# Gate tiles of stick-breaking attention read x before its norm factor, and the second split of x moves behind them

## The chip, the cores and the metric

The kernel runs on one core of a Trainium2 chip. The metric is the device time of one execution in microseconds, the median of several runs. All times below are in microseconds unless they are marked otherwise. A stretch such as "174 to 200" is counted from the first instruction of the profiled execution.

## What is computed

x has 512 tokens of 1024 features, in fp32. A first block has three branches from one normed x: a pooling mixer, a gated linear recurrence and a stick-breaking attention, each weighted by a sigmoid gate. A feed-forward follows, and then two more layers of attention and feed-forward, which the change does not touch. What the change touches is this part of the reference:

```python
h = rms_norm(x, norm_mix[l])                       # x * rsqrt(mean(x*x)) * norm_mix
proj = jnp.einsum('bsd,dc->bsc', h, w_in[l])
u_pool, u_lru, q, k, v, g_logits = jnp.split(proj, splits, axis=-1)
gates = jax.nn.sigmoid(g_logits + b_gate[l]).reshape(B, S, N_BRANCH, D_MODEL)
y_pool = pool_mixer(u_pool, ...)
y_lru = rglru_mixer(u_lru, ..., lru_lambda[l])
qh, kh = rms_norm(q per head), rms_norm(k per head)
y_sb = stick_breaking_attention(qh, kh, vh)        # softplus of the scores, sums along the keys, exp
merged = gates[0]*(y_pool @ w0) + gates[1]*(y_lru @ w1) + gates[2]*(y_sb @ w2)
```

## The kernel before, in words

**Products.** Every fp32 product is made of three matmuls with fp32r operands: each operand is held as a high part and a low part (its rest), and low by high, high by high and high by low are summed in PSUM (lines 313 to 315, `products`). One tile is 128 features by 512 tokens, over 8 slices of the 1024 input features, so 24 matmuls.

**Weights.** They come in chunks of 1 MB. SyncE fetches a chunk into `raw` when GpSimd has finished with the chunk two places earlier. ScalarE makes the high part (line 973, `refill`), in the order of its own program and after the PE has finished with the buffer. GpSimd makes the low part in four pieces (line 853), and the PE waits for each piece. There are two buffers, so a chunk that is refilled late meets the PE two tiles or more later. A chunk holds two tiles of 128 features.

**x.** The first split of x has the gain `norm_mix` but not the factor 1/rms of the token (`rstd`), which isn't known yet. The 16 query and key tiles (feature by token) and the values (token by feature) are made from it, and `rstd` or its transposed copy is applied to the sums. Then the second split is made: VectorE writes x times gain times `rstd` (`x_normed`, line 1601), ScalarE copies it to the high part (`normed`, line 1146), VectorE subtracts (`x_low`, line 1607). The kernel before does this for tiles 0 to 3 between the last value tiles, where the PE has finished with the slices, and for tiles 4 to 7 right after them. Everything later in the block reads the second split.

**Query projection.** For each of 16 tiles the PE makes the product; VectorE scales it (line 1537); ScalarE squares it (line 1136); VectorE splits the square in two (lines 1546 and 1548); and the PE sums it over the features (`qk_sum`, line 536) after the product of a later tile. The buffers of the squares are two deep. ScalarE's refills stand between its squares in one program.

**Values.** Two halves (i), each of two chunks (c) and four token tiles (b). After the first half's first chunk, ScalarE refills, then takes a square root for the norm of q and k (line 1154), then copies the values out of banks 0 to 3 (line 1159), which the second half needs. Between these, VectorE and ScalarE compute small terms from `diff_lambda` and `lru_lambda` (the decay terms, lines 1560 to 1580). In the second half the PE spreads the norm factors (`qk_spread`, line 582) and VectorE applies them (line 1593).

**Attention.** Eight heads. For each head h the PE runs, in this order: the gate tile `sb_gate(h)` (a `g2x` tile, 24 matmuls into bank 7), the scores of head h+1 (line 626), the values of head h-1 (line 652), and the sums of head h (`sb_sums`, lines 638 and 642). ScalarE and VectorE make softplus from the scores (lines 1178 to 1184, and 1628 to 1640, which ends in `sp_ready`); `sb_sums` waits for it. VectorE reads bank 7 after that (line 1645). Before the first head the PE makes the scores of heads 0 and 1. After the last sums come `lru(0)`, the values of head 7, `lru(1)`, and the attention's branch product `sb_branch(0)`.

**Behind it.** Recurrence and branch tiles, then eight pooling tiles, then `g0x` 0 and 1, the pool product (`wp`), and `g0x` 2 and 3, whose chunk ScalarE refills with `mix_refill(16)`; each has a number n in the list `MIX`.

The order on the PE at the start of attention, which the change leaves as it is:

```python
            sb_scores(0)
            sb_scores(1)
            sb_gate(0)
            sb_sums(0)
            for h in range(1, 7):
                sb_gate(h)
                sb_scores(h + 1)
                sb_values(h - 1)
                sb_sums(h)
            sb_gate(7)
            sb_values(6)
            sb_sums(7)
            lru(0)
```

## Time and profile before

| what | before |
|---|---|
| median of 3 runs | 2308.89 us (2307.97 to 2309.07) |
| the profiled execution's own time | 2308.41 us |
| its span, first to last instruction | 2306.7 us |
| PE matmul busy | 2236.3 us (97%) |
| PE weight load busy | 1812.0 us (79%) |
| GpSimd, VectorE, ScalarE busy | 1015.6, 865.5, 813.3 us |
| mean granted clock of the PE | 0.991 |

The shares are for the whole program; the change touches the first 470 us or so. A busy PE in this profile is one with a matmul in flight, and matmuls overlap: one of 512 columns shows 0.39 us, but the next starts 0.23 us after it. Start times are what to compare. The granted clock is 1.00 at 2.4 GHz and 0.50 at 1.2 GHz.

### The profile page before, as it was taken

The page shows a single profiled execution, that of the slowest core. Times are in us where ns is not written, and L with a number is a line of the kernel's source. Part 1 is how long each engine was busy: PE and PEld are TensorE (multiplying, and loading weights), DVE is VectorE, ACT ScalarE, POOL GpSimd, SP SyncE. Part 2 cuts the span into 40 slices and gives each one's busy share as a digit, 9 for nine tenths or more (in the row PEclk, how much of TensorE's full clock was granted, in tenths as well). Part 3 has the DMA queues.
Part 4 walks back from the last instruction along what each step waited for, and adds up shares of the span by engine and source line. Part 5 has one row for each costly group of instructions (what it writes and reads, how often), then busy time and mean ns, then how long its engine had stood idle before and what let it go on. Part 6 is the DMA issues. An engine that isn't in the chain of part 4 may idle for free.

```text
span 2306.7 us, 28303 instructions
## 1 busy us (share of the span) xinstructions
PE 2236.3 (97%) x10138; PEld 1812.0 (79%) x10138; DVE 865.5 (38%) x1286; ACT 813.3 (35%) x1095; POOL 1015.6 (44%) x846
## 2 busy tenths in 40 slices
PE   8998999999999999999988999999998999999997
PEld 6766777788888888888867788888886768888885
DVE  4465456723352111222156543332224546332212
ACT  4235565432243222221145343332223534333321
POOL 4432144555544445554431444445554125445452
PEclk9999999999999999999999999999999999999998
DMA  4221022232223222333221123223233112222222
GB/s 164 86 80 55 37 73 81 92 120 91 92 91 109 91 93 85 100 105 109 101 69 33 56 91 109 91 80 100 99 113 105 27 51 92 101 99 91 82 99 74
DMA packets 33279, 202.83 MB, mean 88 GB/s; under 512 B 3964, under 2 KB 4220, under 8 KB 14780
## 3 DMA queue, kind: packets, MB, share of 16 engines
q1 hardware_dynamic: 30508, 192.94, 24.0%
q0 software_dynamic: 2704, 8.97, 1.4%
q8 instruction: 45, 0.74, 0.1%
q14 instruction: 22, 0.18, 0.0%
HBM read 199.74 MB, written 2.15 MB: 88 GB/s over the span
## 4 chain that ended last, share of the span: by engine, by line
PE 77%; issue 13%; POOL 6%; DVE 2%; ACT 1%; DMA 0%; DVEq 0%; POOLq 0%; SPq 0%; ACTq 0%; PEldq 0%
PE bank L313 23%; PE bank L315 23%; PE bank L314 23%; POOL w_low L853 6%; PE bank L511 3%; PE bank L488 2%; PE bank L498 1%; PE bank L484 1%; PE bank L483 0%; PE bank L342 0%; DMA x_residual<-x 0%; POOL w_low L923 0%; PE bank L462 0%; ACT x_high L1103 0%; DVE qk L1356 0%
## 5 line engine op out<-in xcount | busy, mean ns | idle before, releaser
L853 POOL TENSOR_TENSOR w_low<-raw,w_high 128x512 fp32r<-128x512 f32 (+2 forms) x768 | 965.8, 1289 | 1125.1 <-ACT w_high L973 1125.1
L313 PE MATMUL bank<-x_low,w_high 128*128 128x512 f32 x1728 | 678.5, 393 | 13.1 <-DVE x_low L1527 9.8
L315 PE MATMUL bank<-x_high,w_low 128*128 128x512 f32 x1728 | 674.2, 390 | 0.0
L314 PE MATMUL bank<-x_high,w_high 128*128 128x512 f32 x1728 | 674.0, 390 | 0.0
L973 ACT ACTIVATE w_high<-raw 128x2048 fp32r<-128x2048 f32 (+1 forms) x192 | 344.4, 1794 | 611.5 <-PE bank L315 611.5
L313 PEld LDWEIGHTS bank<-x_low,w_high 128*128 128x128 f32 x1728 | 325.5, 188 | 86.5 <-POOL w_low L923 9.8
L314 PEld LDWEIGHTS bank<-x_high,w_high 128*128 128x128 f32 x1728 | 325.4, 188 | 68.2 <-issue 1.4
L315 PEld LDWEIGHTS bank<-x_high,w_low 128*128 128x128 f32 x1728 | 325.2, 188 | 68.3
L313 PE MATMUL bank<-act_low,w_high 128*128 128x512 f32 x528 | 205.4, 389 | 0.0
L314 PE MATMUL bank<-act_high,w_high 128*128 128x512 f32 x528 | 205.4, 389 | 0.0
L315 PE MATMUL bank<-act_high,w_low 128*128 128x512 f32 x528 | 205.4, 389 | 0.0
L313 PE MATMUL bank<-y_low,w_high 128*128 128x512 f32 x336 | 132.5, 394 | 0.0
L1436 DVE TENSOR_TENSOR temp_b<-temp_a,bank 128x512 f32<-128x512 f32 x66 | 45.4, 687 | 230.3 <-PE bank L315 229.9
L314 PE MATMUL bank<-y_high,w_high 128*128 128x512 f32 x336 | 130.7, 389 | 0.0
L315 PE MATMUL bank<-y_high,w_low 128*128 128x512 f32 x336 | 130.7, 389 | 0.0
L1041 ACT ACTIVATE act_high<-temp_b 128x512 f32 x66 | 41.7, 632 | 216.2 <-DVE temp_b L1436 216.1
L1392 DVE TENSOR_TENSOR gate_scaled<-bank,rstd 128x512 f32<-128x512 f32 x24 | 16.6, 692 | 269.2 <-PE bank L315 269.2
L315 PEld LDWEIGHTS bank<-act_high,w_low 128*128 128x128 f32 x528 | 99.1, 188 | 20.7
L314 PEld LDWEIGHTS bank<-act_high,w_high 128*128 128x128 f32 x528 | 99.1, 188 | 20.6
L313 PEld LDWEIGHTS bank<-act_low,w_high 128*128 128x128 f32 x528 | 99.1, 188 | 20.4
L511 PEld LDWEIGHTS bank<-v_tokens,probs_t 128*128 128x128 f32 x560 | 73.7, 193 | 41.3 <-issue 18.3
L1057 ACT ACTIVATE probs<-probs,small 128x128 f32<-128x128 f32 (+1 forms) x112 | 62.8, 560 | 87.0 <-DVE small L1458 86.5
(242 smaller groups left out, 2454.2 us busy)
## 6 DMA issues: line engine op xcount, KB each, us to landing
raw<-wmain SPq DMA_DIRECT2D x144, 1024.0 KB, 4.8
raw<-wdown SPq DMA_DIRECT2D x48, 704.0 KB, 4.1
bias<-distance_table POOLq DMA_DIRECT2D x28, 256.0 KB, 3.5
raw<-wmain SPq DMA_DIRECT2D x4, 512.0 KB, 8.9
x_residual<-x SPq DMA_DIRECT2D x4, 512.0 KB, 7.7
out<-qk SPq DMA_DIRECT2D x8, 256.0 KB, 2.2
matrices<-mats SPq DMA_DIRECT2D x1, 512.0 KB, 11.9
r_blocks<-rg POOLq DMA_DIRECT2D x1, 512.0 KB, 6.4
```

What stands on the lines that cost most here:

```text
L313: pe.matmul(target, sh, ml, start=start and k == 0, stop=False)
L314: pe.matmul(target, sh, mh, start=False, stop=False)
L315: last = pe.matmul(target, sl, mh, start=False, stop=stop and k == n - 1)
L484: last = pe.matmul(bank[b][:, 0:n], tmpa[half, i, q], qk[half, 11, 0:n], start=False, stop=True)
L488: last = pe.matmul(bank[b][:, 0:n], qs[:, u, q], tile(qk, i + k)[:, 0:n], start=True, stop=True)
L498: last = pe.transpose(bank[4 + b % 2][:, k * P:(k + 1) * P], tq[:, b, k * P:(k + 1) * P], ident)
L511: last = pe.matmul(bank[6 + u][:, b * dh:(b + 1) * dh], pts[:, b % 2, k * P:(k + 1) * P], vt[:, k, cut(c, dh)], start=k == 0, stop=k == b)
L853: pool.tensor_tensor(wl[:, c, part], raw[:, c, part], wh[:, c, part].bitcast(F32), ALU.subtract).then_inc(low_ready, 1)
L973: act.activation(wh[:, c, 0:width], raw[:, c, 0:width], ACT.Copy).then_inc(high_ready, 1)
L1041: act.activation(tile(ah, i * 2 + j), tmpb[:, j, :], ACT.Copy).then_inc(sem("f_high"), 1)
L1057: act.activation(tq[:, b, 0:n], tq[:, b, 0:n], ACT.Exp, bias=nm[:, u, b:b + 1], scale=-1.0, accum_out=rs[:, u, b:b + 1]).then_inc(sem("p_r ...
L1436: dve.tensor_tensor(tmpb[:, j, :], tmpa[:, j, :], bank[2 + j][:, :], ALU.mult)\
```

## The change

Attention's eight gate tiles read the first split of x, and `rstd` is multiplied onto their sums on VectorE; the gate's bias moves into the sigmoid. The second split of x is made after the last head's softplus, slice by slice as the PE finishes with each slice of the last gate tile (`x_used`), and `lru(0)` waits for it. ScalarE's eight copies stand before `sb_weights(7)` and `mix_refill(3)`. The squares' buffers are four deep instead of two, each sum follows its tile by four tiles instead of six, and the last one is issued in the first chunk of the values. The small inputs lie in other places. The decay terms are made during the query projection, at tiles 6 to 9. `mix_refill(16)` is issued before the last pooling tile's copy instead of after it and after a table load.

```diff
-    sq = over("squares", [P, 2, S], 24)
-    sqh = over("square_high", [P, 2, S], 26, F32R)
-    sql = over("square_low", [P, 2, S], 28, F32R)
+    sq = over("squares", [P, 4, S], 24)
+    sqh = over("square_high", [P, 4, S], 28, F32R)
+    sql = over("square_low", [P, 4, S], 32, F32R)
...
-    oh = over("onehot", [32, TW], 16)
-    ad = over("table_add", [ROWS, TW], 18)
-    tt = over("table", [ROWS, TW], 20)
-    rb = over("rel_bias", [32, ROWS + 3], 22)
-    lamb = over("lambda_rows", [P, 4, 64], 23)
+    oh = over("onehot", [32, TW], 36)
+    ad = over("table_add", [ROWS, TW], 37.25)
+    tt = over("table", [ROWS, TW], 38.5)
+    rb = over("rel_bias", [32, ROWS + 3], 39.75)
+    lamb = gs[:, 1, 0:256].rearrange("p (n k) -> p n k", n=4)
...
-                    last = pe.matmul(bank[4][0:16, :], pick_r[:, 15 - t:31 - t], part[:, t % 2, :],
+                    last = pe.matmul(bank[4][0:16, :], pick_r[:, 15 - t:31 - t], part[:, t % 4, :],
...
-                    if t >= 6:
-                        qk_sum(t - 6)
+                    if t >= 4:
+                        qk_sum(t - 4)
...
                         if i == c == 0:
-                            qk_sum(10 + b)
-                        if i == 0 and c == 1 and b < 2:
-                            qk_sum(14 + b)
+                            qk_sum(12 + b)
...
-            def column(kind, t, target, x, x_ready=None):
+            def column(kind, t, target, x, x_ready=None, each=None):
...
+                    if each and k < KT - 1:
+                        last.then_inc(sem(each), 1)
                 last.then_inc(sem("tile"), 1)
...
-                column("g2x", t, 7, mixed, "nl_ready" if t == 0 else None)
+                column("g2x", t, 7, mixed, None, "x_used" if t == 7 else None)
...
-                column("lru", t, t % 2, mixed)
+                column("lru", t, t % 2, mixed, "nl_ready" if t == 0 else None)
...
                     refill(t // 2 % 2, BASE["qk"] + t // 2 + 2)
+                if t == 8:
+                    act.wait_ge(sem("lambda_sums"), 2)
+                    act.activation(t1, col("lru_lambda", 0, 8), ACT.Abs).then_inc(sem("lambda_abs"), 1)
+                    act.wait_ge(sem("lambda_abs"), 1)
+                    act.activation(t1, t1, ACT.Exp, scale=-1.0).then_inc(sem("lambda_exp"), 1)
+                    act.activation(lam2, lam2, ACT.Exp).then_inc(sem("lambda_exp"), 1)
                 act.wait_ge(sem("qk_read"), t + 1)
-                if t >= 2:
-                    act.wait_ge(sem("square_low"), t - 1)
-                act.activation(sq[:, t % 2, :], qk[:, t, :], ACT.Square).then_inc(sem("qk_square"), 1)
-            act.wait_ge(sem("lambda_sums"), 2)
-            act.activation(t1, col("lru_lambda", 0, 8), ACT.Abs).then_inc(sem("lambda_abs"), 1)
-            act.wait_ge(sem("lambda_abs"), 1)
-            act.activation(t1, t1, ACT.Exp, scale=-1.0).then_inc(sem("lambda_exp"), 1)
-            act.activation(lam2, lam2, ACT.Exp).then_inc(sem("lambda_exp"), 1)
-
+                if t >= 4:
+                    act.wait_ge(sem("square_low"), t - 3)
+                act.activation(sq[:, t % 4, :], qk[:, t, :], ACT.Square).then_inc(sem("qk_square"), 1)
...
                     act.wait_ge(sem("v_ready"), 5 * i + b + 2)
                     act.wait_ge(sem("token_copied"), 1)
-                    act.wait_ge(table_stored, 16)
                     act.activation(vt[:, b, i * S:(i + 1) * S], bank[b][:, :], ACT.Copy, scale=token_rstd[:, b:b + 1])\
                        .then_inc(sem("v_read"), 1)
-                    if i == 1:
-                        normed(b)
                 refill(1, n0 + 2 * i + 1)
-            for t in range(NB, KT):
-                normed(t)
...
                 sb_weights(h)
                 if h % 2:
                     mix_refill(h // 2)
-            sb_output(6)
+            for t in range(KT):
+                normed(t)
+                if t == 4:
+                    sb_output(6)
             sb_weights(7)
             mix_refill(3)
             sb_output(7)
...
-                    act.activation(merged[:, t, :], merged[:, t, :], ACT.Sigmoid).then_inc(sem("g2_gate"), 1)
+                    act.activation(merged[:, t, :], merged[:, t, :], ACT.Sigmoid, bias=col("b_gate", 16 + t))\
+                       .then_inc(sem("g2_gate"), 1)
...
                     if t % 2:
                         mix_refill(MIX.index(("pool", t // 2)))
+                if t == KT:
+                    mix_refill(16)
                 if t:
                     act.wait_ge(sem("p_ready_value"), t)
                     act.activation(yh[:, t - 1, :], tmpb[:, (t - 1) % 2, :], ACT.Copy).then_inc(sem("p_high"), 1)
...
-                if kind != "wp":
+                if kind != "wp" and n > 16:
                     mix_refill(n)
...
+            def lambdas():
+
+                dve.wait_ge(inputs_landed, 4 * 16)
+                for k in range(2):
+                    step(dve.tensor_tensor(tmpa[:, 0, 0:64], lamb[:, 2 * k, :], lamb[:, 2 * k + 1, :], ALU.mult))
+                    dve.tensor_reduce(lam2[:, k:k + 1], tmpa[:, 0, 0:64], AX.X, ALU.add).then_inc(sem("lambda_sums"), 1)
+                    dve.wait_ge(sem("lambda_sums"), k + 1)
+                step(dve.tensor_scalar(col("qk_norm", 0, 8), col("qk_norm", 0, 8), 128 ** -0.5, None, ALU.mult))
+                step(dve.tensor_tensor(col("subln", 0, 8), col("subln", 0, 8), col("subln_factor", 0, 8), ALU.mult))
...
+            def decays():
+
+                lam_col = col("lru_lambda", 0, 8)
+                dve.wait_ge(sem("lambda_exp"), 2)
+
+                step(dve.tensor_scalar(t2, t1, 2.0, None, ALU.add))
...
+                step(dve.tensor_tensor(nlam, lam2[:, 1:2], lam2[:, 0:1], ALU.subtract))
+                step(dve.tensor_scalar(nlam, nlam, -LAM_INIT, None, ALU.add))
...
             for t in range(17):
+                if t == 6:
+                    lambdas()
+                if t == 9:
+                    decays()
                 if t < 16:
                     dve.wait_ge(sem("qk_ready"), t + 1)
                     dve.tensor_tensor(qk[:, t, :], bank[QK_BANK[t % 6]][:, :], rstd[:, :], ALU.mult)\
...
-                    if t > 2:
-                        dve.wait_ge(sem("qk_sum"), t - 2)
-                    b = (t - 1) % 2
+                    if t > 4:
+                        dve.wait_ge(sem("qk_sum"), t - 4)
+                    b = (t - 1) % 4
                     dve.tensor_copy(sqh[:, b, :], sq[:, b, :]).then_inc(sem("square_high"), 1)
                     dve.wait_ge(sem("square_high"), t)
...
-            lam_col = col("lru_lambda", 0, 8)
-            for k in range(2):
-                step(dve.tensor_tensor(tmpa[:, 0, 0:64], lamb[:, 2 * k, :], lamb[:, 2 * k + 1, :], ALU.mult))
-                dve.tensor_reduce(lam2[:, k:k + 1], tmpa[:, 0, 0:64], AX.X, ALU.add).then_inc(sem("lambda_sums"), 1)
-                dve.wait_ge(sem("lambda_sums"), k + 1)
...
             def x_normed(t):
 
-                dve.wait_ge(sem("v_ready"), 6 if t < NB else 10)
+                if t < KT - 1:
+                    dve.wait_ge(sem("x_used"), t + 1)
+                else:
+                    dve.wait_ge(sem("tile"), TILE["g2x", 7])
                 if t >= 2:
                     dve.wait_ge(sem("nl_ready"), t - 1)
                 dve.scalar_tensor_tensor(tmpa[:, t % 2, :], xT[:, t, :], col("norm_mix", t), rstd[:, :], ALU.mult,
@@ -1607,18 +1624,8 @@
...
-            for n in range(8):
+            for n in range(16):
                 qk_norm(n)
-            for b in range(NB):
-                x_normed(b)
-                qk_norm(8 + 2 * b)
-                qk_norm(9 + 2 * b)
-                x_low(b)
-            x_normed(4)
-            for t in range(5, KT):
-                x_normed(t)
-                x_low(t - 1)
-            x_low(KT - 1)
...
-                dve.tensor_scalar(merged[:, t, :], bank[7][:, :], col("b_gate", 16 + t), None, ALU.add)\
+                dve.tensor_tensor(merged[:, t, :], bank[7][:, :], rstd[:, :], ALU.mult)\
                    .then_inc(sem("g2x_read"), 1)
 
             for h in range(8):
                 softplus(h)
-                sb_gate(h)
+                if h < 7:
+                    sb_gate(h)
+            x_normed(0)
+            for t in range(1, KT):
+                x_normed(t)
+                x_low(t - 1)
+            x_low(KT - 1)
+            sb_gate(7)
             for t in range(KT):
```

The rest of `decays` is the 13 lines that stood behind the table's sum before, unchanged.

## Rows read from the trace of the kernel before

**Rows 1.** The PE's waits over the whole span: us in total, times, longest.

```profile
PE bank L313 <- DVE x_low L1527: 9.8, 1, 9.8
...
PE bank L638 <- DVE softplus_low L1640: 7.8, 1, 7.8
...
PE bank L313 <- POOL w_low L853: 4.1, 4, 2.7
```

**Rows 2.** Two windows: width, then PE, PEld, DVE, ACT, POOL busy, PEclk, DMA, GB/s.

```profile
144.73:148.15 3.42, 3.42 (x9) 2.64 (x9) 0.82 (x2) 0.00 (x0) 3.42 (x3) 0.50 0.00 0
...
455.35:458.76 3.41, 3.41 (x10) 2.66 (x9) 1.87 (x3) 3.35 (x4) 3.41 (x4) 0.50 0.02 5
```

**Rows 3.** Waits between 28 and 128 us, columns as in Rows 1.

```profile
DVE square_high L1546 <- PE bank L536: 53.5, 14, 13.4
...
PE bank L313 <- POOL w_low L853: 1.4, 3, 0.7
```

**Rows 4.** Timeline, PE, query projection tile 8: start us, us.

```profile
61.75 0.39 PE L315 MATMUL bank<-x_high,w_low 128*128 128x512 f32 x1
62.08 0.50 PE L313 MATMUL bank<-x_low,w_high 128*128 128x512 f32 x1
62.42 0.39 PE L314 MATMUL bank<-x_high,w_high 128*128 128x512 f32 x1
```

**Rows 5.** Timeline, PE, across the two halves of the value projection.

```profile
133.68 0.39 PE L315 MATMUL bank<-w_high,x_low 128*128 128x512 f32 x1
...
135.72 0.39 PE L315 MATMUL bank<-w_high,x_low 128*128 128x512 f32 x1
139.41 0.50 PE L313 MATMUL bank<-w_low,x_high 128*128 128x512 f32 x1 [3.30 <-ACT v_tokens L1159]
...
143.37 1.18 PE L582 MATMUL bank<-qk_rstd_parts,matrices_r 16*128 16x512 f32 x4 [0.95 <-DVE qk_rstd_parts L1587]
```

**Rows 6.** Timeline, ScalarE, values and the first head.

```profile
138.15 0.63 ACT L1154 ACTIVATE gate_scaled<-gate_scaled 16x512 f32<-16x512 f32 x1 [5.58 <-DVE gate_scaled L1583]
...
174.64 1.90 ACT L973 ACTIVATE w_high<-raw 128x2048 fp32r<-128x2048 f32 x1
...
185.16 1.28 ACT L1197 ACT_TABLE_LOAD   x1
```

**Rows 7.** Timeline, PE, first head, a middle head, last head.

```profile
175.75 4.55 PE L626 MATMUL bank<-qk 128*128 128x512 f32 x16 [1.13 <-DVE qk L1593]
179.95 0.58 PE L313 MATMUL bank<-x_low,w_high 128*128 128x512 f32 x1
...
194.69 0.79 PE L638 MATMUL bank<-softplus_high,matrices_r 128*128 128x512 f32 x1 [7.82 <-DVE softplus_low L1640]
...
200.09 0.44 PE L313 MATMUL bank<-x_low,w_high 128*128 128x512 f32 x1
...
261.96 0.48 PE L638 MATMUL bank<-softplus_high,matrices_r 128*128 128x512 f32 x1
...
270.75 2.32 PE L626 MATMUL bank<-qk 128*128 128x512 f32 x8
...
289.10 0.45 PE L313 MATMUL bank<-x_low,w_high 128*128 128x512 f32 x1
```

**Rows 8.** Timeline, VectorE: the second split of x, and the last head's softplus.

```profile
178.47 1.76 DVE L1607 TENSOR_TENSOR x_low<-temp_a,x_high 128x512 fp32r<-128x512 f32 x1
...
184.39 1.47 DVE L1607 TENSOR_TENSOR x_low<-temp_a,x_high 128x512 fp32r<-128x512 f32 x2
...
278.82 1.56 DVE L1640 TENSOR_TENSOR softplus_low<-softplus,softplus_high 128x1024 fp32r<-128x1024 f32 x2
```

**Rows 9.** Timeline, GpSimd, end of attention.

```profile
291.57 4.99 POOL L853 TENSOR_TENSOR w_low<-raw,w_high 128x512 fp32r<-128x512 f32 x4 [18.90 <-ACT w_high L973]
```

**Rows 10.** Timeline, PE: the pool product's first matmul.

```profile
446.62 0.39 PE L313 MATMUL bank<-y_low,w_high 128*128 128x512 f32 x1
```

**Rows 11.** Timeline, ScalarE, the refill after the pool stage.

```profile
451.53 1.91 ACT L973 ACTIVATE w_high<-raw 128x2048 fp32r<-128x2048 f32 x1
```

31 lines of the change are left out of this document (13 added, 18 removed).

## The prediction, as it was put on record

> **What bounds the kernel now.** I read the page first: the PE is busy for 97% of the span, so time can only come from stretches in which it waits or runs at the half clock. The waits of the PE say where: 9.8 us at the start, which the change does not touch; one of 7.8 us for `softplus_low`, at the first `sb_sums`; and four for `w_low`, 4.1 us together, of which the longest, 2.7, stands before `g0x` 2 [rows 1]. The windows show what follows such waits. Behind the longer of them, before 144.73 and before 455.35, the granted clock is 0.50 for 3.4 us: 1.2 GHz in place of 2.4 [rows 2]. Then I read the timeline of each stretch that the change touches, for the start times of the matmuls. Outside these stretches the PE does not wait before 470 us, and what follows is ordered by the PE, so I let a gain here reach the end whole.
>
> **Two measures.** Nine matmuls from 133.68 to 135.72 start 0.227 us apart at full clock; the next starts 3.69 later, with 3.30 shown as idle [rows 5]. Two matmuls across a wait for a piece that is only just late, without any idle shown, start 0.33 and 0.34 apart instead of 0.227 each [rows 4]. So a wait that blocks costs what is shown as idle plus about 0.28, and one just missed costs 0.2.
>
> **Squares four deep, sums two tiles earlier.** VectorE waits 14 times, 53.5 us in total, for the PE's `qk_sum` to free a square's buffer [rows 3]. ScalarE's next square and the refill behind it wait for VectorE, so the refill comes late, and the low part of each chunk reaches the PE just late: in tile 8, two pieces cost 0.2 each [rows 4]. Tiles 8, 10, 12 and 14 have two such pieces each. With four buffers, VectorE at tile t needs the sum of tile t-5, issued after product t-1, so it is free whenever a tile is. The refill then goes at the end of its tile, and gains about 7 us on the PE. That is 8 x 0.2 = 1.6, of which I count 1.5. The first value chunk has three blocked waits, 1.4 us [rows 3], and a missed one: 1.4 + 3 x 0.28 + 0.2 = 2.4. The number of sums is the same. VectorE and ScalarE have room for the moved decay terms: VectorE works under 2 us of each 5.9 us tile, and a query tile read 8 us late is needed six tiles on.
>
> **Decay terms.** The square root before the value copies waits 5.58 us for VectorE, which is at the decay terms [rows 6]. The PE waits 3.30 for the first copy, then 0.95 for the norm factors [rows 5]. With the terms gone, the last sum comes earlier too. The copies are in time: gain 3.69 + 0.34 - 2 x 0.227 = 3.6. The factors come 5.6 earlier and the PE reaches them 3.6 earlier against a wait of 0.95: gone as well, 1.0. With no wait the half clock should not follow: nine matmuls in 3.42 us [rows 2] would take 9 x 0.227 = 2.0, so 1.4.
>
> **Gate tiles from the first split.** Now `sb_gate(0)` starts at 179.95, with small waits inside it; `sb_sums(0)` starts at 194.69, behind a wait of 7.82 and at the half clock; `sb_gate(1)` at 200.09: 20.14 us for gate tile and sums [rows 7]. In a middle head, sums and gate tile take 270.75 - 261.96 = 8.79 [rows 7]. The difference is 11.35. What ends it last is not x itself but ScalarE: its copies of x end at 185.1, then comes its table load [rows 6], then softplus. Its refill at 174.64 takes 1.90 [rows 6]; without a copy of x in front of it, it ends at 176.1, and the table load of 1.28 at 177.4. In a middle head ScalarE's first operation comes about 1 us after the scores start and the second, which needs more scores, 0.9 later; here the first is 0.6 late, so I take the chain as 0.3 late. In a middle head the last low part is done 278.82 + 1.56 - 270.75 = 9.63 after the scores start [rows 7, 8]. From 175.75 [rows 7] that is 185.4, plus 0.3 = 185.7, and the PE comes to the sums at 179.95 + 5.54 = 185.5. A wait of 0.2 that blocks: minus 0.4. So 11.35 - 0.4 = 10.95. If ScalarE were as late as before, the bound on this term is 1.1, the small waits inside the gate tile.
>
> **The second split, moved.** It must be ready for `lru(0)`, which starts at 289.10 [rows 7] and wants slice 7 after 21 matmuls, at 293.9. VectorE is free when the last softplus ends, at 280.38 [rows 8], 3.4 us before the last gate tile ends; ScalarE's copy, 0.63, fits under two VectorE operations. Sixteen operations follow. Two `x_low` take 1.47 where GpSimd is idle, and one takes 1.76 where it works [rows 8]. GpSimd's next chunk starts at 291.57 [rows 9], and `mix_refill(3)` now stands behind the eight copies, so GpSimd is idle here: 280.38 + 16 x 0.74 = 292.2, 1.7 before the need. Cost nothing; if the cover is gone, 14.6 us (below). Late next is `mix_refill(3)`: behind the last copy and `sb_weights(7)` it ends near 295, so GpSimd works at 295 to 300 instead of from 291.57 [rows 9]. The PE wants the chunk after `lru(0)`, the values and `lru(1)`, at 289.10 + 5.4 + 2.3 + 5.4 = 302.2, so that is hidden, and so is the fetch behind it, for a chunk that is wanted two more tile pairs on. But GpSimd now meets VectorE's eight `y_low`, which begin about 1.2 us after these values, at 298: two of them at 1.76 instead of 0.74 make VectorE 2 us late, and `lru_gates(1)` may wait a little: minus 0.3, between 0 and 2.
>
> The Trainium skill says more of this meeting (SBUF — State Buffer, "SBUF: two separate sides"): a VectorE operation with two SBUF inputs and a GpSimd operation that reads SBUF take a port pair by turns, each for a whole instruction. The row agrees: 1.76 is near 0.7 plus most of one GpSimd piece of 1.25. By that rule a fully interleaved split would take 1.95 an operation instead of 1.76, and the rival below would give 2302 instead of 2299.
>
> **The refill before the last pooling copy.** The pool product starts at 446.62 [rows 10], when both `g0x` tiles are done; the refill begins only at 451.53, behind the last pooling tile and a table load [rows 11]; and the PE waits 2.7 [rows 1]. Moved, it begins at 446.7 and its first piece is ready about 450, two before the PE's need: gain 2.7 + 0.3 = 3.0. The half-clock stretch behind it, ten matmuls in 3.41 [rows 2], gives 1.3. VectorE's last pooling operations meet GpSimd now, 1 us each, but the second pool product is 12 us off.
>
> **Nothing:** the gate's multiply in place of the add on VectorE, the bias in the sigmoid, the other places of the small inputs, the later wait for the stored table, the eight waits of `lru(0)` when they are met (four or five such waits inside `sb_gate(0)` showed no gap).
>
> **Sum:** 1.5 + 2.4 + 3.6 + 1.0 + 1.4 + 10.95 - 0.3 + 3.0 + 1.3 = 24.9. Against the profiled execution's own time, 2308.41, that is 2283.5. The median of the runs is 0.5 above that execution, so I predict 2284.0.
>
> **Rivals.**
> - The split blocks `lru(0)`. If VectorE met GpSimd throughout, 16 x 1.76 from 280.38 ends at 308.5: 14.6 too late, plus 0.3 and a half clock of 1.4: 2284 + 16 = 2300. For it: the pace in the first split region was that. Against: GpSimd has nothing to do there. A milder form: if the chain began only when the last gate tile ends (283.8), it would end at 295.6 and cost 2. Chance 0.09.
> - The first `sb_sums` still waits long enough to lose the clock. A wait near 2.7 us did so [rows 1, 2]. If ScalarE is that late, 2.7 and 2.2 at half clock: 2289. Against: nothing stands before its table load but a refill. Chance 0.08.
> - Refills come no earlier, because they wait for something else, the fetch for instance. Then 1.5 + 2.4 + 3.0 + 1.3 = 8.2 is lost: 2292. Chance 0.05.
> - Slower: the same place, `lru(0)`, at a pace that eats all. It decides when the wait reaches 24.9 - 1.7 = 23.2, that is (13.5 + 23.2) / 16 = 2.3 us for each operation. At 2.6 the time is 2284 + 28.1 + 1.7 = 2314. No row is near that. Chance 0.02.
> - The change only moves the wait: what leaves `sb_sums(0)` returns at `lru(0)`, and the refills gain nothing, 2308.5. The slack of 1.7 speaks against it. Chance 0.02.
>
> **Numbers.** The forecast's own chance is 0.74. Its terms are known to some 0.5 each; the clock terms (2.7 together, and 2.2 inside the 10.95) could fall otherwise, and the PE's wait of 1.13 before the first scores [rows 7] stays, so a half clock could start there. The range takes in the second rival and the mild form of the first: 2281.0 to 2289.5. A difference of 0.2%, 4.6 us, is about what a measurement of this kernel can tell from none. Faster 0.96, same 0.02, slower 0.02.
>
> **What would show it.** In the profile after: no wait for `w_low` before 130 us and none near 450; no wait for `v_tokens` or `qk_rstd_parts`; `sb_gate(0)` without gaps, then under 0.5 us of wait for `softplus_low`; `lru(0)` without a wait for `x_low`, with the last `x_low` 1 to 2 us before slice 7; granted clock 1.00 from 15 to 1100 us. A wait for `x_low` at `lru(0)` of over 2 us, or softplus on ScalarE starting over 2 us after the scores, would make it wrong.

## Result, and the profile after

The kernel after takes 2285.79 us, the median of four runs (2284.23 to 2289.18); before, run beside it, takes 2308.98 (2307.97 to 2314.33). The ratio is 0.9898, with a 95% interval of 0.9886 to 0.991: 1.0% faster. The prediction was 2284.0, with a range of 2281.0 to 2289.5. The execution that was profiled took 2289.18, the longest of the four.

The page of the kernel after, span, the PE's busy time, its granted clock in 40 slices, and the chain that ended last:

```profile
span 2287.5 us, 28298 instructions
...
PE 2231.9 (98%) x10138; PEld 1811.3 (79%) x10138; DVE 856.5 (37%) x1286; ACT 814.8 (36%) x1095; POOL 1012.7 (44%) x846
...
PEclk9999999999999999999999999999999999999998
...
PE 94%; DVE 4%; ACT 1%; issue 1%; DMA 0%; DVEq 0%; SPq 0%; ACTq 0%; PEldq 0%
```

The PE works nearly as long as before, 4.4 us less; the span is 19.2 shorter. What went is mostly idle time, and the chain shows it: before, the PE held 77% of it, issue 13% and GpSimd 6%; now the PE holds 94%.

The PE's waits over the whole span, after (us in total, times, longest), the rows to hold against [rows 1]:

```profile
PE bank L313 <- DVE x_low L1529: 9.6, 1, 9.6
PE bank L511 <- DVE probs_t L1469: 9.3, 9, 1.5
PE bank L498 <- ACT probs L1057: 4.8, 1, 4.8
...
PE bank L313 <- ACT temp_a L1289: 1.2, 1, 1.2
PE bank L624 <- DVE qk L1607: 1.1, 1, 1.1
```

The waits for `softplus_low`, `w_low`, `v_tokens` and `qk_rstd_parts` are gone. Between 28 and 455 us two are left (and one of 0.3): 1.1 before the first scores, which was there before [rows 7], and 1.2 for `temp_a`, which is new. The PE's timeline at the points of the prediction's sum, against [rows 5, 7]:

```profile
165.12 4.55 PE L624 MATMUL bank<-qk 128*128 128x512 f32 x16 [1.12 <-DVE qk L1607]
...
174.99 0.46 PE L636 MATMUL bank<-softplus_high,matrices_r 128*128 128x512 f32 x1
...
178.22 0.45 PE L313 MATMUL bank<-x_low,w_high 128*128 128x512 f32 x1
...
267.25 0.45 PE L313 MATMUL bank<-x_low,w_high 128*128 128x512 f32 x1
...
272.11 0.39 PE L313 MATMUL bank<-x_low,w_high 128*128 128x512 f32 x1
...
431.52 0.50 PE L313 MATMUL bank<-x_low,w_high 128*128 128x512 f32 x1 [1.16 <-ACT temp_a L1289]
...
535.03 0.39 PE L313 MATMUL bank<-lru_low,w_high 128*128 128x512 f32 x1
```

Read down, these are the scores of head 0, its sums (no idle in the row), `sb_gate(1)`, `lru(0)`, slice 7 of `lru(0)`, `g0x` 2, and the first product with `lru_low`. In the kernel before, that last one stands here:

```profile
559.97 0.39 PE L313 MATMUL bank<-lru_low,w_high 128*128 128x512 f32 x1
```

The first matmul of the span starts at 9.79 us before and at 9.64 after. From it to the first product with `lru_low`, a stretch called M below, it is 559.97 - 9.79 = 550.18 before and 535.03 - 9.64 = 525.39 after: 24.8 us shorter, against 24.9 predicted. The PE's stretch behind it has the same products and nearly the same waits in both (`probs_t` 9.4 and 9.3, `probs` 4.8 and 4.8), yet it is 5.7 longer in the profiled execution of after: 24.8 + 0.15 - 5.7 = 19.2. The windows say what it did there (width; PE, PEld, DVE, ACT, POOL busy; PEclk; DMA share; GB/s). After:

```profile
1139.40:1142.80 3.40, 3.40 (x8) 2.10 (x9) 1.30 (x6) 2.12 (x5) 3.40 (x3) 0.51 0.00 0
1160.00:1163.40 3.40, 3.40 (x10) 2.50 (x11) 1.44 (x5) 1.64 (x6) 0.00 (x0) 0.50 0.00 0
165.00:180.00 15.00, 14.88 (x72) 11.80 (x73) 9.55 (x18) 11.22 (x23) 6.02 (x6) 1.00 0.38 141
```

The last row is the first head at full clock, as forecast. The first two are stretches behind 1100 us in which the clock is at 0.50, 1.2 GHz in place of 2.4, while the PE is busy throughout. The PE has come out of a wait just before each; the one before the first row:

```profile
1139.31 4.08 PE L488 MATMUL bank<-qk,q_stage 128*128 128x128 f32 x8 [2.13 <-PEq L336]
```

Before has nearly the same waits there, but not a stretch of half clock behind each. After has six of 3.4 us between 500 and 2260 us, 20.4 in all, and none before 1139; before has one of 3.4 and one of 6.8. In 10.2 us more at half clock the PE does what takes 5.1 at full clock, so they are worth 5.1 of the 5.7.

### The profile page after: what moved, and what is told of

Its sections match the earlier page's. It is cut to its first block, busy times and chain, and to the rows that moved or that the text cites. A ratio compares the mean times of both kernels' runs of the same rounds, so it can differ in the third digit from the quotient of the medians.

```text
span 2287.5 us, 28298 instructions
## 1 busy us (share of the span) xinstructions
PE 2231.9 (98%) x10138; PEld 1811.3 (79%) x10138; DVE 856.5 (37%) x1286; ACT 814.8 (36%) x1095; POOL 1012.7 (44%) x846
## 4 chain that ended last, share of the span: by engine, by line
PE 94%; DVE 4%; ACT 1%; issue 1%; DMA 0%; DVEq 0%; SPq 0%; ACTq 0%; PEldq 0%
PE bank L313 27%; PE bank L315 27%; PE bank L314 27%; PE bank L511 3%; PE bank L488 2%; PE bank L498 1%; PE bank L636 1%; PE bank L624 1%; PE bank L650 1%; DVE pool_a L1723 1%; PE bank L484 1%; DVE temp_b L1533 0%; PE bank L483 0%; PE bank L582 0%; PE bank L536 0%
## 5 line engine op out<-in xcount | busy, mean ns | idle before, releaser
L313 PE MATMUL bank<-x_low,w_high 128*128 128x512 f32 x1728 | 676.7, 392 | 10.8 <-DVE x_low L1529 9.6
```

Source lines behind the costliest of these rows:

```text
L313: pe.matmul(target, sh, ml, start=start and k == 0, stop=False)
```

## Experiments

All kernels issue the same 10138 matmuls, in the same order but for the sums of squares, which take a product's time wherever they stand. So the start of each, counted from the first matmul, can be set against the same one of the kernel after. The table, worked out from the starts in each trace, gives how much later than in after the PE gets through each section (us; a minus is earlier). The sections end, in after, at 58 us (start and first query tiles), 106 (query projection), 163 (values), 169 (first scores), 193 (first head and `sb_gate(1)`), 275 (other heads and `lru(0)`) and 444 (pool stage and `g0x` 2); their sum is the difference in M. "Own time" is that of the profiled execution, "rest" the time from the end of M to the start of the last matmul, and "half" the time at half clock between 500 and 2260 us (each kernel also ends in 14 to 17 us at half clock, which that column leaves out). Nothing behind M is edited in any kernel, and each computes the same values as after. A kernel with one profiled execution and no median named below ran once.

| kernel | own time | start | projection | values | scores | head | `lru(0)` | pool | M | rest | half |
|---|---|---|---|---|---|---|---|---|---|---|---|
| before | 2308.41 | 0.35 | 1.63 | 8.51 | 0.00 | 11.22 | 0.00 | 3.09 | 24.80 | 1733.5 | 10.2 |
| a0 same again | 2289.03 | -0.01 | 0.00 | 0.00 | 0.00 | -0.03 | 0.00 | 0.00 | -0.04 | 1739.2 | 20.4 |
| a1 decay terms back | 2283.99 | 0.02 | 0.00 | 0.00 | 0.00 | -0.01 | 0.00 | 0.01 | 0.02 | 1733.6 | 10.2 |
| a2 squares back | 2294.43 | 0.00 | 6.47 | 2.30 | 1.69 | -0.09 | 0.00 | 0.00 | 10.36 | 1734.6 | 13.6 |
| a3 pool refill back | 2288.68 | -0.18 | 0.00 | 0.00 | 1.68 | -0.08 | 0.00 | 3.15 | 4.57 | 1733.9 | 6.8 |
| b1 split back | 2298.13 | 0.35 | 0.00 | 0.00 | 0.00 | 11.22 | 0.00 | -0.02 | 11.55 | 1736.6 | 17.0 |
| b2 gate tiles alone | 2302.18 | 0.64 | 1.63 | 8.49 | 1.69 | -0.07 | 0.00 | 3.11 | 15.47 | 1736.5 | 17.0 |
| b3 normed x twice | 2291.71 | 0.66 | 0.00 | 0.00 | 1.69 | -0.10 | 5.93 | 0.00 | 8.18 | 1733.3 | 6.8 |
| b4 refill inside | 2287.33 | 0.40 | 0.00 | 0.00 | 0.00 | 0.00 | 2.05 | -0.02 | 2.44 | 1734.8 | 13.6 |
| c1 sigmoid first | 2287.11 | 0.10 | 0.00 | 0.00 | 0.00 | -0.01 | 0.00 | -1.47 | -1.37 | 1738.4 | 17.0 |
| c2 scores first | 2290.01 | 0.06 | 0.00 | 0.00 | -1.17 | 6.25 | 0.00 | 0.01 | 5.15 | 1734.9 | 13.6 |
| c3 both | 2285.59 | -0.13 | 0.00 | 0.00 | -1.17 | 4.57 | 0.00 | -1.47 | 1.80 | 1733.6 | 6.8 |
| d1 both, refill later | 2284.06 | 0.07 | 0.00 | 0.00 | -1.17 | -0.08 | 0.00 | -1.47 | -2.65 | 1736.6 | 17.0 |

Two columns move by chance. The start differs by -0.2 to 0.7 between kernels with the same code there. In the scores, 1.68 or 1.69 appears in four kernels that share that code with the others: a half-clock stretch of 3.4 us behind the wait of 1.1. In a3 and b3 nothing ahead of the scores is edited, so there it is no effect of the edit; for a2 and b2, which are edited ahead of them, that is likely but not shown. Everywhere else a section that was not edited agrees to 0.03, or to 0.10 in the head behind such a stretch. So each edit's price can be read from its own column.

In a1 to b2 the theory to be tested is the prediction's sum, term by term; its rivals put the same gain down to another part of the change. In b3 and b4 it is the slack at `lru(0)`. In c1 to d1 it is whether the two waits that are left can be taken out, and what that costs.

**a0, the kernel after once more.** No edit.

> The changed kernel once more, unaltered. Its first 460 us gained 24.9 us on the PE against before, and the profiled execution then lost 5.7 of them in half-clock stretches between 1140 and 1806 us, where no code differs. Theory A (where those stretches fall is left to chance in each execution): the time from the PE's first matmul to its first product with lru_low is again 525.4 us within 0.2, but the number of half-clock stretches behind 500 us differs from the profiled execution's six, and the total lies at 2284 to 2287. Theory B (the changed kernel's own order brings them about): the same stretches at the same places, and a total near 2289.

Its profiled execution took 2289.03, with the six stretches of half clock where after has them, within 1 us. The other runs took 2286.43, 2285.32 and 2289.41; the median is 2287.73, the ratio 0.9907 [0.989, 0.9923]. The mean granted clock of the runs goes with their times: 0.992 at 2289.03 and 2289.41, 0.993 at 2286.43, 0.995 at 2285.32, and in the four of after 0.992 at 2289.18, 0.993 at 2286.06, 0.994 at the other two. So the 5.7 us are not a fixed price of the change: the same program runs without most of them. Both theories got a part: the profiled execution looks like B, and two of the four runs fall in A's 2284 to 2287. That the two profiled executions agree to the microsecond is left unexplained.

**a1, decay terms back behind the query tiles.** The two new functions are called where their lines stood before, and ScalarE's three operations too.

```diff
-                if t == 6:
-                    lambdas()
-                if t == 9:
-                    decays()
...
             dve.sem_inc(table_ready, 1)
+            lambdas()
+            decays()
```

> The changed kernel with the decay terms back behind the table's sum. Theory A (the terms add up): the PE waits about 3 us for v_tokens at the start of the second value half and about 1 for the norm factors, and runs a half-clock stretch of 3.4 us; first matmul to first lru_low product 525.4 + 6.0 = 531.4. Theory B (with the last sum of squares earlier, VectorE is early enough even so): under 1.5 us, below 527.

No section differs. VectorE's timeline around the decay terms in a1:

```profile
112.88 0.29 DVE L1542 TENSOR_TENSOR temp_a<-gate_scaled 128x64 f32<-128x64 f32 x1
...
117.69 1.17 DVE L1559 SCALAR_TENSOR_TENSOR small<-small 128x8 f32<-128x8 f32 x6
...
120.11 0.15 DVE L1566 TENSOR_SCALAR small<-small 128x1 f32<-128x1 f32 x1
121.32 0.68 DVE L1596 TENSOR_SCALAR gate_scaled<-bank 16x512 f32<-16x512 f32 x1 [1.06 <-PE bank L536]
```

and the same wait in the kernel after:

```profile
120.81 0.68 DVE L1597 TENSOR_SCALAR gate_scaled<-bank 16x512 f32<-16x512 f32 x1 [8.51 <-PE bank L536]
```

The terms take from 112.88 to 120.26, and then VectorE still waits 1.06 us for the last sum. In after, with nothing to do, it waits 8.51 for the same sum. The terms were late before because VectorE reached them late, at 126.6, held up by the sums. They also took longer there, 10.8 us up to 137.4 in place of 7.4, since GpSimd worked beside them from 131.4: six small operations took 3.30 in place of 1.17. The moved sums alone bring them early enough, and moving them too is worth nothing.

**a2, the squares two deep and the sums two tiles later again.**

```diff
-                    if t >= 4:
-                        qk_sum(t - 4)
+                    if t >= 6:
+                        qk_sum(t - 6)
...
-                    if t > 4:
-                        dve.wait_ge(sem("qk_sum"), t - 4)
-                    b = (t - 1) % 4
+                    if t > 2:
+                        dve.wait_ge(sem("qk_sum"), t - 2)
+                    b = (t - 1) % 2
```

> The changed kernel with two square buffers and each sum six tiles behind, as before. Theory A: waits for w_low return at the first value chunk (1.4 us in three) and just-missed pieces in tiles 8 to 14; 525.4 + 3.9 = 529.3 to the first lru_low product. It could be more, since VectorE now has the decay terms in this stretch: 530. Theory B (the late refills have another cause, the fetch): no change, 525.4.

The projection and the values cost 6.47 + 2.30 = 8.8, where the sum's terms for the squares are 3.9; neither theory had that much. The waits between 28 and 128 us in a2, the rows to hold against [rows 3]:

```profile
DVE square_high L1585 <- PE bank L536: 52.5, 12, 13.4
...
PE bank L313 <- POOL w_low L855: 4.5, 5, 1.8
```

`w_low` costs 4.5 in five waits, where before had 1.4 in three, and the half clock follows at 99 us. VectorE's timeline in a2 shows why it is worse than before:

```profile
84.73 0.79 DVE L1585 CAST square_high<-squares 128x512 fp32r<-128x512 f32 x1 [4.58 <-PE bank L536]
...
87.14 1.25 DVE L1554 TENSOR_SCALAR small<-small 128x8 f32<-128x8 f32 x1
...
91.89 0.69 DVE L1576 TENSOR_TENSOR qk<-bank,rstd 128x512 f32<-128x512 f32 x1
```

The decay terms now stand between the tiles. With two buffers VectorE comes to them only after a sum has released it, at 84.73, and they hold up the next `qk` copy until 91.89; it didn't have to wait for its product by then. ScalarE's next square waits 9.98 us for that copy, the refill queued behind the squares is late with it, and the PE waits. So the decay terms and the squares have to be judged together: in the query projection the terms cost nothing with four buffers (after) and hold everything up with two.

**a3, the refill back behind the pooling copies.**

```diff
-                if t == KT:
-                    mix_refill(16)
...
-                if kind != "wp" and n > 16:
+                if kind != "wp":
```

> The changed kernel with the refill after g0x 0 and 1 back behind the last pooling copy and the table load. Theory A: the wait of 2.7 for w_low returns in place of the 1.2 us for ScalarE's sigmoid, with a half-clock stretch: 525.4 + 1.5 + 1.5 = 528.4. Theory B (the half clock before had to do with the earlier stretches): no half clock, 526.9.

The pool stage costs 3.15, and the whole of it has the wait for `w_low` of 2.7 and its half clock in place of the wait for `temp_a` of 1.2. Windows of a3:

```profile
166.00:169.40 3.40, 3.40 (x9) 2.07 (x8) 0.00 (x0) 2.65 (x5) 3.40 (x4) 0.55 0.00 0
436.10:439.40 3.30, 3.30 (x10) 2.53 (x9) 1.75 (x3) 2.43 (x3) 3.30 (x3) 0.50 0.00 0
```

The second row is the stretch that was expected. The first is the one of the scores, which no edit touches.

**b1, the second split back before the first head.** Copies of x on ScalarE beside the value copies, the split on VectorE between the norm multiplies, `sb_gate` from the second split, bias in the add.

```diff
-                column("g2x", t, 7, mixed, None, "x_used" if t == 7 else None)
+                column("g2x", t, 7, mixed, "nl_ready" if t == 0 else None)
...
+                    if i == 1:
+                        normed(b)
```

> The changed kernel with the gate tiles reading the second split, made among the last value tiles as before. Theory A (ScalarE's copies of x put softplus off): the wait for softplus_low at the first sums is back at 7 to 8 us, with a half clock behind it; 525.4 + 11 = 536.4 us from the first matmul to the first lru_low product. Theory B (softplus of head 0 was late for another reason, the decay terms or the refills): under 3 us of wait, 528 to 530.

The first head costs 11.22, to the hundredth what it costs before; the prediction's term was 10.95. The wait and the clock behind it in b1:

```profile
PE bank L636 <- DVE softplus_low L1654: 7.8, 1, 7.8
```

```profile
179.10:189.20 10.10, 4.70 (x18) 4.51 (x19) 9.49 (x18) 5.72 (x13) 0.00 (x0) 0.50 0.09 33
```

The wait is the 7.8 of [rows 1]. It ends at 184.50, so the half clock begins inside it and goes on behind it; the PE is busy for 4.70 of these 10.1 us.

**b2, the gate tiles alone.** The edits of a1, a2 and a3 together, so that only the moved split is left of the change.

> The kernel before with only the gate tiles and the second split moved (decay terms, squares and the pool refill as before). Theory A (the parts are independent): it gains 11, so 550.2 - 11 = 539.2 to the first lru_low product. Theory B (the parts help each other): a gain of under 8, above 542.

The head is as in after, and all that before pays elsewhere is paid: 1.63 in the projection, 8.49 in the values, 3.11 in the pool stage. The waits for `w_low`, 4.1, and `v_tokens`, 3.3, are those of [rows 1]. The gain in M is 24.80 - 15.47 = 9.3: the edit's 11.2 and 0.1, less the 1.69 of the scores and 0.3 of the start. M by itself lies between theory A's 11 and theory B's 8; the head's own column is what bears out A.

**b3, normed x made twice.** VectorE writes each piece of normed x two times, the same value, so that the chain before `lru(0)` is 8 x 0.79 = 6.3 us longer (0.75 an operation, and its gap).

```diff
+                step(dve.scalar_tensor_tensor(tmpa[:, t % 2, :], xT[:, t, :], col("norm_mix", t), rstd[:, :],
+                                              ALU.mult, ALU.mult))
```

> The changed kernel with each of VectorE's eight multiplications of the second split issued twice, the second writing the same again. In the profile after, the last x_low ends at 270.1 and lru(0) wants slice 7 at 272.3. Theory A (the split is covered by 2.2 us of slack and VectorE's pace decides): 8 x 0.75 = 6 us more for VectorE, the PE waits in lru(0) and loses 6 - 2.2 + 0.3 = 4.1, or 5.5 if the half clock follows: 529.5 to 531. Theory B (lru(0) is held by something other than VectorE, or has more slack): under 2, below 527.4.

`lru(0)` costs 5.93. The three matmuls of it that wait in b3:

```profile
273.65 0.47 PE L313 MATMUL bank<-x_low,w_high 128*128 128x512 f32 x1 [0.91 <-DVE x_low L1626]
...
275.80 0.50 PE L313 MATMUL bank<-x_low,w_high 128*128 128x512 f32 x1 [1.22 <-DVE x_low L1626]
...
278.13 0.47 PE L313 MATMUL bank<-x_low,w_high 128*128 128x512 f32 x1 [1.37 <-DVE x_low L1626]
```

By the starts of the matmuls these waits cost 4.2, 3.5 of it idle, and a half-clock stretch behind them, at 279 us, another 1.7. The chain is 6.3 longer and costs 4.2, so the slack is 2.1. Read directly in after: the last `x_low` ends at 270.1 and slice 7 starts at 272.11, so 2.0. The prediction had 1.7.

**b4, the refill inside the split.** `mix_refill(3)` goes from behind the eight copies to the third.

```diff
+                if t == 2:
+                    mix_refill(3)
                 if t == 4:
                     sb_output(6)
             sb_weights(7)
-            mix_refill(3)
```

> The changed kernel with mix_refill(3) between ScalarE's third and fourth copies of x instead of behind all eight, so that GpSimd works while VectorE makes the second half of the split. ScalarE is busy 1.9 us longer there. Theory A (a VectorE operation with two SBUF inputs waits for GpSimd's, 1.76 instead of 0.74 each): about five operations at 1.76 and ScalarE's 1.9, together 5 to 7 us late against 2.2 of slack; the PE loses 3 to 5 in lru(0), 528.5 to 530.5. Theory B (the two don't hold each other here): under 1, below 526.4.

`lru(0)` costs 2.05: two waits of 0.89 and 0.58 with 0.28 each, and no half clock follows them. That is under theory A's 3 to 5 and over theory B's 1. VectorE's and GpSimd's timelines in b4:

```profile
266.69 1.59 DVE L1619 SCALAR_TENSOR_TENSOR temp_a<-x_residual,columns,rstd 128x512 f32<-128x512 f32 x1
268.20 1.78 DVE L1625 TENSOR_TENSOR x_low<-temp_a,x_high 128x512 fp32r<-128x512 f32 x1
```

```profile
264.65 6.48 POOL L853 TENSOR_TENSOR w_low<-raw,w_high 128x512 fp32r<-128x512 f32 x4 [13.30 <-ACT w_high L973]
```

Where GpSimd works, VectorE's two operations take 1.59 and 1.78, as against 0.75 and 0.69 in the kernel after:

```profile
267.97 0.75 DVE L1618 SCALAR_TENSOR_TENSOR temp_a<-x_residual,columns,rstd 128x512 f32<-128x512 f32 x1
268.64 1.47 DVE L1624 TENSOR_TENSOR x_low<-temp_a,x_high 128x512 fp32r<-128x512 f32 x2
```

Four of the sixteen are stretched (1.47, 1.59, 1.78, 1.59), and the last `x_low` comes 4.0 us later than in after, not 5 to 7; less the slack of 2.0, that is the 2.05. So the place of the refill behind the copies is what makes the long split fit under the last gate tile. The Trainium skill (SBUF — State Buffer, "SBUF: two separate sides") has the two engines take a port pair by turns, each for a whole instruction. The rows agree in part: the operations of GpSimd stretch too, 6.48 for four in place of 5.00, but 1.59 and 1.78 stay under the 0.75 + 1.25 and 0.69 + 1.25 that strict turns would make of the times alone.

**c1, the pool's sigmoid first.** ScalarE's table load and the first two sigmoids of `g0x` go ahead of the last pooling copy, since these sigmoids free the banks that `g0x` 2 writes.

```diff
                 if t == KT:
                     mix_refill(16)
+                    act.preload_act_table(ACT.Sigmoid)
+                    for j in range(2):
+                        act.wait_ge(sem("tile"), TILE["g0x", j])
+                        act.activation(tmpa[:, j, :], bank[4 + j][:, :], ACT.Sigmoid,
+                                       bias=col("b_gate", j)).then_inc(sem("gate_ready"), 1)
...
-            act.preload_act_table(ACT.Sigmoid)
...
-                if kind[2:] == "x":
+                if kind[2:] == "x" and n > 16:
```

> The changed kernel with the sigmoid's table load and the two sigmoids of g0x 0 and 1 moved in front of the last pooling copy on ScalarE. Theory A (g0x 2 waits for the sigmoid to free its bank, and ScalarE stood waiting for VectorE's last pooling tile): the 1.2 us wait goes, 525.4 - 1.3 = 524.1. Theory B (the pieces of w_low come just as late): the wait stays in another name, above 525.

The pool stage is 1.47 shorter and no wait for `temp_a` is left. This is the wait that the prediction overlooked. ScalarE's timeline in the kernel after:

```profile
424.96 1.92 ACT L973 ACTIVATE w_high<-raw 128x2048 fp32r<-128x2048 f32 x1 [3.11 <-PE bank L315]
428.83 0.63 ACT L1268 ACTIVATE y_high<-temp_b 128x512 fp32r<-128x512 f32 x1 [1.95 <-DVE temp_b L1728]
429.49 1.28 ACT L1270 ACT_TABLE_LOAD   x1
430.78 1.27 ACT L1289 ACTIVATE temp_a<-bank,columns 128x512 f32<-128x512 f32 x2
```

The refill that was moved is done at 426.9; then ScalarE sits 1.95 us behind VectorE's last pooling operation, loads its table, and starts the sigmoid at 430.78. `g0x` 2 wants its bank at 430.2.

The 1.95 us behind VectorE have a cause of their own. VectorE's last pooling operation in the kernel after, where the moved refill has set GpSimd to work from 426.96:

```profile
427.01 1.79 DVE L1728 SCALAR_TENSOR_TENSOR temp_b<-pool_a,pool_u 128x512 f32<-128x512 f32 x1
```

and the same one in the kernel before, with GpSimd idle:

```profile
448.86 0.69 DVE L1714 SCALAR_TENSOR_TENSOR temp_b<-pool_a,pool_u 128x512 f32<-128x512 f32 x1
```

It takes 1.1 us more, and the copy, the table load and the sigmoid stand in line behind it. An estimate from these rows: without the meeting the sigmoid would start near 429.7, and nearly all of the wait of 1.2 would be gone. No run takes the meeting away alone.

**c2, the first scores as soon as their own norms are there.** The scores of head 0 wait for 2 normed pieces of q and k instead of 16, those of head 1 for 14; the first gate tile waits for all 16. ScalarE's last refill of the values goes from in front of the first softplus to behind it.

```diff
-                    pe.wait_ge(sem("qk_normed"), 16)
+                    pe.wait_ge(sem("qk_normed"), 14 if h else 2)
...
-                if t:
-                    pe.wait_ge(sem("g2x_read"), t)
+                pe.wait_ge(*((sem("g2x_read"), t) if t else (sem("qk_normed"), 16)))
...
-                refill(1, n0 + 2 * i + 1)
+                if i == 0:
+                    refill(1, n0 + 1)
...
             softplus(0)
+            refill(1, n0 + 3)
             softplus(1)
```

> The changed kernel with the scores of heads 0 and 1 waiting only for the norms that they read and the banks that they write (2 and 14 of 16 instead of 16), the gate tile 0 for all 16, and ScalarE's refill behind the first softplus instead of before it. Theory A: the 1.1 us wait before the scores goes (1.3 in all) and softplus keeps up: 524.1 to the first lru_low product. Theory B (softplus of head 0 is now what ends last, and the wait only moves to the first sums): no gain, 525.4.

The wait of 1.1 is gone, 1.17 gained in the scores, and 6.25 lost in the first head, which neither theory had. The PE's wait in c2:

```profile
PE bank L636 <- DVE softplus_low L1648: 2.9, 1, 2.9
```

VectorE and GpSimd in c2:

```profile
171.30 2.00 DVE L1645 CAST softplus_high<-softplus 128x1024 fp32r<-128x1024 f32 x2
173.34 3.60 DVE L1648 TENSOR_TENSOR softplus_low<-softplus,softplus_high 128x1024 fp32r<-128x1024 f32 x2
```

```profile
171.53 6.55 POOL L852 TENSOR_TENSOR w_low<-raw,w_high 128x512 fp32r<-128x512 f32 x4 [17.74 <-ACT w_high L972]
```

The refill behind `softplus(0)` hands GpSimd its work at 171.5, just as VectorE splits the softplus. The two casts take 2.00 and the two low parts 3.60. The PE waits 2.9, and the clock is at a half for 6.8 us from 178.

**c3, both edits.**

> Both of the two edits above on the changed kernel. Theory A: they add up, 522.8 us to the first lru_low product, and the total is 2282 to 2284.5, 1.1% under the kernel before. Theory B (one of them fails): 524.1 or more, total 2285.

The two gains stand, 1.17 and 1.47, and the wait of 2.9 costs 4.57 here, with 3.4 us of half clock behind it in place of c2's 6.8. Theory B came out, at a higher price than it named. The median of four runs is 2286.41, ratio 0.9906 [0.989, 0.9923], no better than after.

**d1, both, and the refill behind the second softplus.**

```diff
             softplus(0)
-            refill(1, n0 + 3)
             softplus(1)
+            refill(1, n0 + 3)
             sb_weights(0)
```

> The changed kernel with both edits (sigmoids before the last pooling copy; scores of heads 0 and 1 as early as their norms allow), and ScalarE's refill behind the second softplus instead of behind the first. Behind the first, GpSimd's low part ran against VectorE's cast and subtraction of head 0, which took 5.6 us instead of 2.5, and the PE waited 2.9. Theory A (that meeting is the whole of the loss): no wait for softplus_low over 0.3 at the first sums; first matmul to first lru_low product 525.4 - 1.4 - 1.3 = 522.7. Theory B (softplus of head 0 itself is too late once the scores come 1.3 earlier): a wait near 1, 523.7 or more. The total hangs on where half-clock stretches fall behind 1100 us, in either theory: 2281 to 2286, and in any one execution they may take back what this gains.

The same four operations in d1:

```profile
171.45 0.90 DVE L1649 CAST softplus_high<-softplus 128x1024 fp32r<-128x1024 f32 x2
172.38 1.56 DVE L1652 TENSOR_TENSOR softplus_low<-softplus,softplus_high 128x1024 fp32r<-128x1024 f32 x2
```

```profile
175.61 2.85 POOL L852 TENSOR_TENSOR w_low<-raw,w_high 128x512 fp32r<-128x512 f32 x2 [21.67 <-ACT w_high L972]
```

0.90 and 1.56 with GpSimd idle until 175.61, against 2.00 and 3.60 in c2. Both gains stand and nothing is lost: M is 2.65 below after, and the PE waits for nothing between 28 and 455 us. The meeting itself isn't gone: GpSimd now works from 175.61 to 181.5, and the two casts of head 1 take 2.96 in place of 0.90, but no wait of the PE follows. The median of four runs is 2283.84 (2283.45 to 2285.14), the ratio 0.9888 [0.9871, 0.9904]. It is the lowest median here, but the interval takes in that of after: shown is the shorter M, not a faster total.

## Why the prediction was right

**The sum held.** The row of before in the table is the sum, measured: 0.35 at the start, which is chance; 1.63 in the projection (predicted 1.5); 8.51 in the values (2.4 + 3.6 + 1.0 + 1.4 = 8.4); 11.22 in the first head (10.95); nothing at `lru(0)` (nothing); 3.09 in the pool stage (3.0 + 1.3 = 4.3); nothing at `y_low` (minus 0.3). The total of 24.8 against 24.9 is closer than its terms: 0.35 of start and 0.8 in four other terms make up for the 1.2 that the pool stage gave less.

**Squares and decay terms: the size right, the attribution wrong.** The buffers did what was forecast. VectorE has no wait for a square's buffer left between 28 and 128 us, and its longest in total is for the products themselves:

```profile
DVE qk L1574 <- PE bank L315: 36.7, 12, 4.6
```

But the prediction priced the squares at 3.9 and the decay terms at 6.0 with the clock. Undone alone, the terms cost 0.0 (a1) and the squares 8.8 (a2); undone together they cost 10.1 (b2), what before pays. So moving the terms is worth 1.4 while the squares are two deep, and nothing once they are four. The step that failed is "the square root before the value copies waits 5.58 us for VectorE, which is at the decay terms". True as a row [rows 6], but VectorE was at them so late because the sums had held it. With the sums earlier the terms have 8.5 us of idle time to stand in, and at their old place they take 7.4. The total came out because both edits are in it.

**Gate tiles from the first split: right.** The scores start at 165.12 and the PE meets the sums at 174.99 without idle; the last `softplus_low` is ready at 174.9, that is 9.8 after the scores' start. The forecast was 9.95 and a wait of 0.2. Undone alone (b1) or done alone (b2) the edit is worth 11.2 to 11.3. The rival of a first sum that still waits is out. The path was the forecast one as well. ScalarE's table load in front of the first softplus, in the kernel after:

```profile
165.41 1.28 ACT L1193 ACT_TABLE_LOAD   x1
```

Softplus starts 1.6 us after the scores, as the prediction worked out; in before and in b1 it starts 10.7 behind them. One thing the prediction left out: ScalarE's last four copies of x waited 6.1 us for VectorE's products of x in before, so it was the pair of them that was late, and no run takes one away without the other.

**The second split, moved: right.** The sixteen operations run at 0.75 and 0.69, GpSimd idle beside them; the slack is 2.0 (forecast 1.7). Both sides of it were tested: 6.3 more work makes it block (b3), and so does GpSimd at the same time (b4). The rival in which the split blocks `lru(0)` is a real mechanism with the condition that the prediction gave it, and the condition is not met. The rival in which the wait only moves is out: M would not have changed. The meeting with `y_low` came, and cost nothing where 0.3 was counted. VectorE's eight in the kernel after, the first of them behind ScalarE's copy:

```profile
276.44 5.85 DVE L1667 TENSOR_TENSOR y_low<-qk,y_high 128x512 fp32r<-128x512 f32 x8 [5.73 <-ACT y_high L1212]
```

They take 5.85 us, 4.91 in the kernel before; nothing of it reached the PE.

**Refill before the last pooling copy: the mechanism right, the size 1.2 too large.** The term of 3.0 and 1.3 was 3.1. The wait for `w_low` of 2.7 went, and its half clock, but a wait of 1.2 that costs 1.47 came. The step that was mis-sized is "VectorE's last pooling operations meet GpSimd now, 1 us each, but the second pool product is 12 us off". The meeting came, 1.1 us on the last operation, but what waits for it was followed to the pool product alone. ScalarE's copy waits for it too, behind the copy stand a table load and the first sigmoid, and the bank of `g0x` 2 is held until that sigmoid has read it. c1 takes the sigmoid out of this line, and then the two edits give 3.09 + 1.47 = 4.6 where 4.3 was forecast for the refill.

**Clock behind 500 us: not in the sum.** "I let a gain here reach the end whole" failed for the profiled execution by 5.7; the median of the runs came out 1.8 above the forecast. With half of the column "half" taken off, the rest is 1728.4 us in before and 1729.0 in after, so the clock accounts for all but 0.6 of the 5.7. Over all fourteen profiled executions the same sum gives 1727.8 to 1730.5, so it holds to some 3 us only. Each of the 50 stretches between 500 and 2260 us begins inside a wait of the PE or less than 1.5 us behind one, and all fourteen executions have nearly the same waits of 0.8 us and more there, 4.8 the longest. What differs is how many of these waits get one: the 4.8 always, the 2.1 in eight of fourteen, one of 1.4 in three. Why is open. The experiments leave the code behind 500 us alone, and when the PE reaches it doesn't decide alone: a1 and after get there at the same M, and have 10.2 and 20.4.

**Two slips that changed nothing.** The half clock at 144.73 is told as behind one of the longer waits for `w_low`; what stands in front of it are the wait of 3.30 for `v_tokens` and, 1.4 us ahead, that of 0.95 [rows 5]. And the rival at `lru(0)` comes to 2300, not to 2299; at 1.95 us an operation it is 2303.

## What to carry to other kernels

Before lateness is put down to the work that an engine is at, ask what made it come to that work late; a wait upstream made 7 us of small operations look costly that fit into idle time once it was gone. When a stall is removed, walk the resource list of the instruction that stalled (its weights, its input, its bank) and find what is late next: here it was the bank, and over a quarter of the term. When an edit makes two engines meet, follow the stretched operation to everything that waits for it, not only to the PE's next use of its result. In this kernel a long VectorE chain with little slack is safe only where GpSimd is idle, so the refill that wakes GpSimd belongs behind it.

## What the runs showed of the hardware

The granted clock drops to 0.50 for 3.4 us, at times for 6.8 or 10.2, and the PE can be busy throughout, as from 1160.00 to 1163.40 in after. In the fourteen profiled executions there are 65 such stretches between 20 and 2260 us, and every one begins inside a wait of the PE or less than 1.5 us behind one, the shortest of these waits 0.82 us. Most waits of 0.8 us and more, 192 of 257, have none. In this kernel on one core it goes with 4 us from one run to another of the same program (a0, 2285.32 to 2289.41, with the mean clock from 0.995 to 0.992). The wait of 1.1 us in front of the first scores is followed by it in a2, a3, b2 and b3, for 1.69 us each time, and not in before, after, a0, a1, b1, b4 and c1. What decides was not settled.

A cast from SBUF to SBUF, one input only, is stretched beside GpSimd as much as an operation with two inputs: 2.00 us for two that take 0.90 alone (c2 and d1), and 3.60 in place of 1.56 for the two with two inputs.
